# First slot of a hybrid decoder layer reordered, GpSimd given a share of its weight split, prefetch buffers re-laid

## The chip, the cores and the metric

The kernel runs on one core of a Trainium2 chip. The metric is device time in microseconds (us) from launch to end. The kernel before takes 1367.12 us, the median of 3 runs (1366.63 to 1367.73).

## What is computed

One decoder layer on 256 tokens of width 1024, in float32, then a mixture of experts (MoE) and a last RMSNorm. Cut to what matters here:

```
h = rmsnorm(x, norm_mix);  proj = h @ w_in                  # 1024 x 10256
y_ml = mLSTM(conv + silu of q,k; v; gates);  y_fx = forgetting attention
kv = rmsnorm(mem, norm_mem) @ w_mem_kv;      y_ca = attention of q into kv
x += (sum over b of sigmoid(gate_b) * (y_b @ w_branch[b])) @ w_out
t = rmsnorm(x, norm_moe);  top 4 of 32 experts by softmax router
for each expert:  u = t @ w1 + b1;  a = clamped SwiGLU(u);  out += weight * (a @ w2 + b2)
return rmsnorm(x, norm_final)
```

Each expert has 8 MB in `w_exp_in` and 4 MB in `w_exp_out`, 12 MB in all.

## The kernel before

Every engine has its own program, and semaphores join them. The work has two parts.

**Mixing.** The dense matmuls are 32 units of 512 weight columns (`UNITS`), each cut into 2 slots (`SLOTS`, 64 in all, numbered i). SyncE (SP) loads unit u into `ring[u % 3]`, 2 MB each. For accuracy each operand is split into a rounded part `hi` and a remainder `lo`, and three products are summed: hi·hi, hi·lo, lo·hi. For slot i ScalarE (ACT) writes `w_hi[i % 2]` (`round_weights`, L571), then VectorE (DVE) writes `w_lo[i % 2]` (`split_weights`, L870), then TensorE (PE) runs the slot (`project`: L1286 for slots of kind "T", L1297 for kind "N"). `round_weights(i)` waits until slot i-2 is done, because the two buffers alternate. Slot 0 goes down the list k = 0..7 with all three products of a k together. Beside the slots the dictionary `STAGES` hangs small pieces of work on slot numbers: `conv` and `conv_silu` on slots 0 to 7, `gate_weights` on slot 2, `gates` (PE, L1325) on slot 3, the attention heads later.

**The start.** SP loads x (2 transfers), small rows, unit 0 in two halves, three transfers of gate weights `wg`, three of biases, unit 1, `mem`, unit 2. ACT sums squares of x (`square_sums`, L545) and takes one Sqrt for both halves of tokens (L547). DVE takes reciprocals (L850), scales x into `xn` (`scale_rows`, L852) and copies `cols` (the norm weights, turned by PE at L1246). PE turns `xn` (`turn_rows`, L1233) into banks 4 to 7, ACT rounds them to `h_hi` (`round_turned`, L555), DVE forms `h_lo` (`split_turned`, L859). PE fills gaps with dummy matmuls (`keep_clock`, L1240). Right after slot 1's weights are rounded ACT sums the squares of `mem` (`square_sums(mems, ...)`), ahead of `round_weights(2)`. GpSimd (POOL) builds constants, at the end `pick` (a memset L489 and two `affine_select`, L493).

**MoE.** 10 buffers `place[0..9]` of 2 MB hold pieces of expert weights, 6 pieces to an expert: 4 of `w_exp_in` and 2 of `w_exp_out`, in turn. SP loads a piece (`load`, L390) once PE has used up the place (`place_used`). PE runs an expert at L1472/L1473 and adds results by L1557. The first 10 pieces are loaded ahead, during mixing. The places lie over the mixing buffers, so that each waits for the buffers under it to be dead: place 0 to 2 are the ring, place 3 is `fxkT` and `fxv`, and the layout order of `part(...)` decides the others.

Of the kernel before, what the change touches and what calls it, by code (L numbers as in the profile page):

```python
# [7 lines left out]
ALU = mybir.AluOpType  # L8
# [128 lines left out]
def build(nc, x, mem, norm_mix, w_in, b_ml_gates, conv_ml, ml_head_norm, b_fx_gate, norm_mem,  # L137
# [3 lines left out]
    with ctx:  # L141
# [117 lines left out]
        cF = part("cF", [12, S])  # L259
        big_f = part("big_f", [P, 2 * D])  # L260
        sig_o = big_f[:, :].rearrange("p (t d) -> p t d", t=TT)
        ycaT = big_f[:, :].rearrange("p (c s) -> p c s", c=KT)

        o_hi, o_lo = (part(f"o_{n}", [P, KT, S], F32R) for n in ("hi", "lo"))

        h_hi, h_lo = (part(f"h_{n}", [P, KT, S], F32R) for n in ("hi", "lo"))

        w_hi = [part(f"w_hi{n}", [P, KT, HW], F32R) for n in range(2)]
        w_lo = [part(f"w_lo{n}", [P, KT, HW], F32R) for n in range(2)]
        mixing.close()  # L270
# [103 lines left out]
        def _(sp):  # L374
# [5 lines left out]
            def load(e, j, b):  # L380
# [9 lines left out]
                sp.dma_start(place[b][:, :, :].rearrange("p k n -> p (k n)"), src).then_inc(place_in[b], 16)  # L390

            for u, (name, kind, j) in enumerate(UNITS):
                b = u % RING
                if u == 21:

                    sp.wait_ge(proj_done, FIRST["caq"] + 3)
                    load(0, RING, RING)
                if u == 25:

                    sp.wait_ge(proj_done, FIRST["caq"] + 11)  # L400
                    load(0, W1, W1)
# [63 lines left out]
        def _(pool):  # L465
# [65 lines left out]
        def _(act):  # L531
# [9 lines left out]
            def square_sums(src, n, loaded):  # L541

                for t in range(TT):
                    act.wait_ge(loaded[t], 16)
                    act.activation(square_dump[t], src[:, t, :], ACT.Square, accum_out=ss[:, t, 0:1]).then_inc(squares, 1)  # L545
                act.wait_ge(squares, 2 * n + 2)
                act.activation(std[:, :, 0:1], ss[:, :, 0:1], ACT.Sqrt, bias=eps[:, 0:1],  # L547
                               scale=1.0 / D).then_inc(std_ready, 1)

# [9 lines left out]
            def round_weights(i):  # L559
                if i >= len(SLOTS):  # L560
                    return
                u = UNIT_OF[i]
                if i == 0:
                    act.wait_ge(first_half_in, 16)
                else:
                    act.wait_ge(weights_in[u % RING], 16 * (u // RING + 1))
                if i >= 2:
# [271 lines left out]
        def _(dve):  # L839
# [8 lines left out]
            def scale_rows(src, dst, n):  # L848
                dve.wait_ge(std_ready, n + 1)
                step(dve.reciprocal(rstd[:, :, 0:1], std[:, :, 0:1]))  # L850
                for t in range(TT):
                    dve.tensor_scalar(dst[:, t, :], src[:, t, :], rstd[:, t, 0:1], None, ALU.mult).then_inc(scaled, 1)  # L852

# [11 lines left out]
            def split_weights(i):  # L865
                if i >= len(SLOTS):
                    return
                dve.wait_ge(weights_rounded, i + 1)
# [4 lines left out]
            scale_rows(xs, xn, 0)  # L873
# [188 lines left out]
            for i in range(len(SLOTS)):  # L1062
# [22 lines left out]
            dve.tensor_reduce(sq[:, :], ss[:, :, 0:2], AX.X, ALU.add).then_inc(sq_ready, 1)  # L1085
            dve.wait_ge(std_ready, 3)
            dve.reciprocal(rstd[:, :, 0:1], std[:, :, 0:1]).then_inc(rstd_ready, 1)
# [131 lines left out]
        def _(pe):  # L1219
# [7 lines left out]
            def turn_rows(src, user):  # L1227

                for q in range(4):
# [16 lines left out]
            pe.transpose(bank[7][:, 0:64], rows[:, :], ident[0:64, 0:64]).then_inc(filled[7], 1)  # L1246
            keep_clock(0, 8)
            pe.wait_ge(scaled, 2)
            turn_rows(lambda t, c: xn[:, t, P * c:P * (c + 1)], "x")
            keep_clock(0, 8)  # L1250
            def free_banks(i):
# [8 lines left out]
                else:  # L1260
                    pe.wait_ge(act_drained, act_drains(last))

            def project(i):
                name, kind, j, half = SLOTS[i]

                pe.wait_ge(weights_split, i + 1)
                free_banks(i)
                if j == 0 and half == 0:
# [324 lines left out]
```

## Time and profile before

| | |
|---|---|
| median of 3 runs | 1367.12 us |
| the profiled execution, its own time | 1366.06 us |
| its span, first to last instruction | 1364.3 us |
| PE busy | 1317.0 us, 97% of the span |
| DVE / ACT / POOL busy | 473.9 / 327.5 / 21.4 us |
| chain that ended last | PE 81%, DMA 13%, ACT 2%, DVE 1% |
| mean granted TensorE clock | 0.995 |
| traffic | 475.06 MB, mean 348 GB/s |

All times below are of that one execution, in us from the first instruction. A row of a timeline gives start, duration, engine, line and operation, count, and in brackets how long the engine had been idle and what released it. The mixing part runs to about 437, the experts from 448 to 1351.

### The profile page before, as it was taken

Reading aid. Unit: us, or ns where it says so; the run is one execution under the profiler, and the core shown is the slowest. Engines: PE = TensorE matmul, PEld = TensorE weight load, DVE = VectorE, ACT = ScalarE, POOL = GpSimd, SP = SyncE. Lnnn points to the kernel's source line nnn. Section 1 sums busy time; section 2 is a strip of 40 time slices with the busy share of each in tenths; the row PEclk is TensorE's granted clock in tenths of the full one; section 3 lists DMA queues with packets and bytes.
Section 4 is the critical chain, followed back from the end, with each engine's and each line's share of the span. In section 5 each row is a group of like instructions: output and inputs, shape, how many; then the busy total and the mean of one; then the engine's idle time right before and its main releaser. Section 6 shows DMA issues by size and latency. Waiting matters only on the chain.

```text
span 1364.3 us, 16054 instructions
## 1 busy us (share of the span) xinstructions
PE 1317.0 (97%) x6489; PEld 679.6 (50%) x6489; DVE 473.9 (35%) x802; ACT 327.5 (24%) x476; POOL 21.4 (2%) x39
## 2 busy tenths in 40 slices
PE   7999999999999999999999999999999999999995
PEld 7889997988888333333333333333333333333331
DVE  4754545444656322322223222322223222322223
ACT  5564545464444100110011000100011001110002
POOL 2000000000101000000000000000000000000000
PEclk9999999999999999999999999999999999999998
DMA  9354443545568999999999999999999999999993
GB/s 315 138 198 160 139 170 124 211 160 211 185 244 331 407 427 430 432 431 430 431 432 431 431 431 431 433 431 430 431 432 430 431 431 431 434 430 431 432 430 160
DMA packets 68233, 475.06 MB, mean 348 GB/s; under 512 B 8480, under 2 KB 10592, under 8 KB 43616
## 3 DMA queue, kind: packets, MB, share of 16 engines
q1 hardware_dynamic: 66048, 473.01, 83.7%
q10 hardware_dynamic: 2144, 1.47, 0.4%
q8 instruction: 29, 0.48, 0.1%
q14 instruction: 12, 0.10, 0.0%
HBM read 473.42 MB, written 1.05 MB: 348 GB/s over the span
## 4 chain that ended last, share of the span: by engine, by line
PE 81%; DMA 13%; ACT 2%; DVE 1%; SPq 1%; issue 1%; ACTq 0%; DVEq 0%
PE bank L1472 44%; PE bank L1297 17%; DMA place<-in_w_exp_in 12%; PE bank L1286 7%; PE bank L1557 4%; PE bank L1485 1%; ACT fxqT L808 1%; PE bank L1529 1%; PE bank L1501 1%; DMA fxv<-in_mem 1%; PE bank L1521 1%; PE bank L1473 1%; PE bank L1410 1%; PE bank L1429 1%; DVE w_lo L870 1%
## 5 line engine op out<-in xcount | busy, mean ns | idle before, releaser
L1472 PE MATMUL bank<-place,fxqT 128*64 128x512 f32 x1536 | 688.0, 597 | 22.1 <-ACT fxqT L808 15.6
L1473 PE MATMUL bank<-place,fxqT 128*64 128x512 f32 x1536 | 688.1, 597 | 0.0
L1472 PEld LDWEIGHTS bank<-place,fxqT 128*64 128x64 f32 x1536 | 199.2, 137 | 422.1 <-issue 389.6
L1148 DVE TENSOR_SCALAR big_a<-bank 128x512 f32<-128x512 f32 x32 | 22.1, 692 | 525.2 <-PE bank L1473 525.2
L870 DVE TENSOR_TENSOR w_lo<-ring,w_hi 128x2048 fp32r<-128x2048 f32 x64 | 146.7, 2291 | 153.5 <-ACT w_hi L571 153.3
L1473 PEld LDWEIGHTS bank<-place,fxqT 128*64 128x64 f32 x1536 | 199.2, 137 | 0.0
L571 ACT ACTIVATE w_hi<-ring 128x2048 fp32r<-128x2048 f32 x64 | 122.7, 1918 | 158.7 <-PE bank L1297 113.9
L805 ACT ACTIVATE big_a<-big_a 128x512 f32<-128x512 f32 x32 | 20.1, 630 | 435.3 <-DVE big_a L1148 435.3
L1176 DVE TENSOR_TENSOR xs<-bank,xs 128x512 f32<-128x512 f32 x132 | 81.9, 683 | 24.3 <-PE bank L1557 24.3
L1297 PE MATMUL bank<-w_hi,h_hi 128*128 128x512 f32 x224 | 88.3, 394 | 0.1
L1297 PE MATMUL bank<-w_hi,h_lo 128*128 128x512 f32 x224 | 87.3, 390 | 0.0
L1297 PE MATMUL bank<-w_lo,h_hi 128*128 128x512 f32 x224 | 87.2, 389 | 0.0
L815 ACT ACTIVATE p_a<-bank 128x512 f32<-128x512 f32 x32 | 19.1, 598 | 245.4 <-PE bank L1473 245.4
L1286 PE MATMUL bank<-h_hi,w_hi 128*128 128x256 f32 x256 | 74.2, 290 | 3.0 <-DVE w_lo L870 3.0
L1286 PE MATMUL bank<-h_hi,w_lo 128*128 128x256 f32 x256 | 73.1, 286 | 0.0
L1286 PE MATMUL bank<-h_lo,w_hi 128*128 128x256 f32 x256 | 73.1, 285 | 0.0
L1557 PE MATMUL bank<-p_a,fxqT 64*128 64x512 f32 x264 | 65.6, 615 | 0.8 <-ACT p_a L815 0.8
L1473 PE MATMUL bank<-big_c,sel 128*64 128x512 f32 x132 | 62.1, 592 | 0.0
L1472 PE MATMUL bank<-big_c,sel 128*64 128x512 f32 x132 | 62.1, 592 | 0.0
L1139 DVE TENSOR_TENSOR fxqT<-bank,g_rows 128x256 f32<-128x256 f32 x66 | 24.9, 419 | 95.0 <-PE bank L1485 95.0
L1286 PEld LDWEIGHTS bank<-h_hi,w_hi 128*128 128x128 f32 x256 | 49.8, 195 | 3.4 <-DVE w_lo L870 3.2
L1297 PE MATMUL bank<-w_hi,o_hi 128*128 128x512 f32 x128 | 51.0, 398 | 0.0
(269 smaller groups left out, 1272.6 us busy)
## 6 DMA issues: line engine op xcount, KB each, us to landing
place<-in_w_exp_in SPq DMA_DIRECT2D x128, 2048.0 KB, 28.2
place<-in_w_exp_out SPq DMA_DIRECT2D x64, 2048.0 KB, 28.5
ring<-in_w_in SPq DMA_DIRECT2D x19, 2048.0 KB, 7.6
ring<-in_w_branch SPq DMA_DIRECT2D x6, 2048.0 KB, 7.6
ring<-in_w_mem_kv SPq DMA_DIRECT2D x4, 2048.0 KB, 7.7
ring<-in_w_out SPq DMA_DIRECT2D x2, 2048.0 KB, 12.4
ring<-in_w_in SPq DMA_DIRECT2D x2, 1024.0 KB, 7.5
xs<-in_x SPq DMA_DIRECT2D x2, 512.0 KB, 4.3
```

Of the source, the lines that this page charges most:

```text
L571: act.activation(hi, whole, ACT.Copy).then_inc(weights_rounded, 1)
L805: act.activation(sig, gate, ACT.Sigmoid, scale=ALPHA).then_inc(sig_ready, 1)
L815: act.activation(yS, bank[5][:, :], ACT.Copy).then_inc(yS_ready, 1)
L870: dve.tensor_tensor(lo, whole, hi.bitcast(F32), ALU.subtract).then_inc(weights_split, 1)
L1139: dve.tensor_tensor(gotT[:, :, h, :], bank[3][:, :].rearrange("p (q h c) -> p q h c", q=4, h=2)[:, :, h, :], weights[:, :, h].unsqueeze(2) ...
L1148: dve.tensor_scalar(gate.rearrange("c (q p) -> c q p", q=4), bank[0][:, :].rearrange("c (p q) -> c q p", q=4), LIMIT, None, ALU.min).then_ ...
L1176: dve.tensor_tensor(dst, bank[b][:, :], dst, ALU.add).then_inc(put_added, 1)
L1286: ins = mm(bank[i % 4][:, S * c:S * (c + 1)], stationary, moving, start=(k == 0 and n == 0), stop=(k == KT - 1 and n == 2))
L1297: ins = mm(bank[2 * (UNIT_OF[i] % 2) + c][:, :], stationary, moving, start=(k == 0 and n == 0), stop=(k == KT - 1 and n == 2))
L1472: mm(o[0:CAP, :], lhsT, low, start=start, stop=stop)
L1473: return mm(o[CAP:P, :], lhsT, high, start=start, stop=stop)
L1557: mm(bank[b][:, :], selWT[half, t, :], yS[half, :], start=True, stop=True).then_inc(put_done, 1)
```

## The change

Seven edits:

1. On slot 0, DVE writes `w_hi` itself (`tensor_copy`), POOL writes the first half (k = 0..3) of `w_lo`, DVE the second half. ACT's first weight rounding is now that of slot 1. POOL's build of `pick` comes behind its new work.
2. `project_first`: PE runs slot 0 product by product: all hi·hi, then all with `h_lo`, then all with `w_lo`.
3. RMSNorm's Sqrt, reciprocal and scaling go by half of the tokens. `turn_x` turns the first half of the tokens for all 4 banks, then the second. Two runs of dummy matmuls go, one shrinks from 8 to 4.
4. `cols` is copied ahead of the scaling of x.
5. SP loads units 1 and 2 and `mem` ahead of `wg` and the biases.
6. The squares of `mem` (ACT) and its scaling (DVE) move to slot 3.
7. The mixing buffers are laid out anew: place 4 is now `big_b` and `big_f`, place 5 `o_hi`/`o_lo`, place 6 `h_hi`/`h_lo`, place 7 the weight buffers of even slots, place 8 those of odd slots, place 9 `big_e`, `pick` and the masks. The loads ahead follow: places 3, 9, 4, 2, 5, 0, 1, 7, 6, 8, where it was 3, 4, 5, 6, 2, 0, 1, 7, 8, 9.

The semaphores `weights_rounded` and `weights_split` no longer count slot 0, so the waits on them ask for one less.

DVE at the start, before (`w_lo0` is the buffer of slot 0, `w_lo1` that of slot 1; bank 7 holds the turned rows):

```order
L850 RECIPROCAL rstd<-std 128x2
L852 TENSOR_SCALAR big_a<-xs,rstd 128x1024 x2
L875 COPY cols<-bank7 128x64
L870 TENSOR_TENSOR w_lo0<-ring0,w_hi0 128x2048
L859 SCALAR_TENSOR_TENSOR h_lo<-bank4,cols,h_hi 128x256 x2
L859 SCALAR_TENSOR_TENSOR h_lo<-bank5,cols,h_hi 128x256 x2
L859 SCALAR_TENSOR_TENSOR h_lo<-bank6,cols,h_hi 128x256 x2
L859 SCALAR_TENSOR_TENSOR h_lo<-bank7,cols,h_hi 128x256 x2
L870 TENSOR_TENSOR w_lo1<-ring0,w_hi1 128x2048
```

and DVE at the start, of the change:

```order
L887 COPY cols<-bank7 128x64
L864 RECIPROCAL rstd<-std 128x1
L865 TENSOR_SCALAR big_a<-xs,rstd 128x1024
L864 RECIPROCAL rstd<-std 128x1
L865 TENSOR_SCALAR big_a<-xs,rstd 128x1024
L891 CAST w_hi0<-ring0 128x2048
L872 SCALAR_TENSOR_TENSOR h_lo<-bank4,cols,h_hi 128x256 x2
L872 SCALAR_TENSOR_TENSOR h_lo<-bank5,cols,h_hi 128x256 x2
L872 SCALAR_TENSOR_TENSOR h_lo<-bank6,cols,h_hi 128x256 x2
L872 SCALAR_TENSOR_TENSOR h_lo<-bank7,cols,h_hi 128x256 x2
L895 TENSOR_TENSOR w_lo0<-ring0,w_hi0 128x1024
L883 TENSOR_TENSOR w_lo1<-ring0,w_hi1 128x2048
```

The copy of `cols` moved up, the rounding of slot 0's weights came from ACT, and half of their remainder went behind `h_lo`.

SP's loads ahead of the experts, from the two loads of `w_out` (units 30 and 31) on, before:

```order
L415 DMA ring0<-in_w_out 128x8x512
L415 DMA ring1<-in_w_out 128x8x512
L390 DMA place6<-in_w_exp_in 128x4096
L390 DMA place2<-in_w_exp_in 128x4096
L390 DMA place0<-in_w_exp_in 128x4096
L390 DMA place1<-in_w_exp_in 128x4096
L390 DMA place7<-in_w_exp_in 128x4096
L390 DMA place8<-in_w_exp_in 128x4096
L390 DMA place9<-in_w_exp_in 128x4096
```

and there of the change:

```order
L422 DMA ring0<-in_w_out 128x8x512
L422 DMA ring1<-in_w_out 128x8x512
L391 DMA place2<-in_w_exp_in 128x4096
L391 DMA place5<-in_w_exp_out 128x4096
L391 DMA place0<-in_w_exp_in 128x4096
L391 DMA place1<-in_w_exp_in 128x4096
L391 DMA place7<-in_w_exp_in 128x4096
L391 DMA place6<-in_w_exp_in 128x4096
L391 DMA place8<-in_w_exp_in 128x4096
```

Seven pieces follow `w_out` in both; place 2 now goes first and no longer waits for slot 59, and place 7 waits for slot 62 where it waited for slot 63.

The diff, cut to its core:

```diff
+        big_f = part("big_f", [P, 2 * D])
 ...
+        o_hi, o_lo = (part(f"o_{n}", [P, KT, S], F32R) for n in ("hi", "lo"))
+        h_hi, h_lo = (part(f"h_{n}", [P, KT, S], F32R) for n in ("hi", "lo"))
+        w_parts = [[part(f"w_{n}{i}", [P, KT, HW], F32R) for n in ("hi", "lo")] for i in range(2)]
+        w_hi, w_lo = ([pair[n] for pair in w_parts] for n in range(2))
 ...
@@ SP @@
-                    load(0, RING, RING)
+                    load_ahead(3)
-                    load(0, W1, W1)
+                    load_ahead(9)
-                    load(0, W1 + 1, W1 + 1)
+                    load_ahead(4)
+                if u == RING:
+                    sp.wait_ge(first_low, 1)
                 if u >= RING:
-                    sp.wait_ge(weights_split, 2 * (u - RING) + 2)
+                    sp.wait_ge(weights_split, 2 * (u - RING) + 1)
 ...
-                if u == 0:
+                if u == 2:
                     wv = w_in[0].rearrange("(k p) n -> p k n", p=P)
                     sp.dma_start(wg[:, :, 0:4], wv[:, :, C_F:C_F + 4]).then_inc(gatew_in, 16)
 ...
+            last = len(UNITS) - 1
+            sp.wait_ge(weights_split, SLOT_OF[last - 2, 1])
+            load_ahead((last - 2) % RING)
             sp.wait_ge(proj_done, FIRST["b2"] + 4)
-            load(1, 0, PIECES)
-            for u in range(len(UNITS) - RING, len(UNITS)):
-                sp.wait_ge(weights_split, SLOT_OF[u, 1] + 1)
-                load(0, u % RING, u % RING)
+            load_ahead(5)
+            for u in (last - 1, last):
+                sp.wait_ge(weights_split, SLOT_OF[u, 1])
+                load_ahead(u % RING)
+            sp.wait_ge(proj_done, len(SLOTS) - 1)
+            load_ahead(7)
             sp.wait_ge(proj_done, len(SLOTS))
-            for j in range(1, W1):
-                load(1, j, PIECES + j)
+            load_ahead(6)
+            load_ahead(8)
@@ POOL @@
+            pool.wait_ge(rows_zero, 4)
+            pool.wait_ge(first_rounded, 1)
+            whole, hi, lo = slot_weights(0)
+            pool.tensor_tensor(lo[:, 0:KT // 2, :], whole[:, 0:KT // 2, :], hi[:, 0:KT // 2, :].bitcast(F32),
+                               ALU.subtract).then_inc(first_low, 1)
+            pool.wait_ge(first_low, 1)
             pool.memset(pick[:, :, :].bitcast(F32), 0.0).then_inc(pick_built, 1)
@@ ACT @@
-                act.wait_ge(squares, 2 * n + 2)
-                act.activation(std[:, :, 0:1], ss[:, :, 0:1], ACT.Sqrt, bias=eps[:, 0:1],
+                    act.wait_ge(squares, 2 * n + t + 1)
+                    act.activation(std[:, t, 0:1], ss[:, t, 0:1], ACT.Sqrt, bias=eps[:, 0:1],
 ...
-            round_weights(0)
 ...
-            act.wait_ge(scaled, 2)
-            square_sums(mems, 1, [mem_in, mem_in])
 ...
+                if i == 3:
+                    square_sums(mems, 1, [mem_in, mem_in])
@@ DVE @@
+            scale_rows(xs, xn, 0)
+            dve.wait_ge(first_half_in, 16)
+            whole, hi, lo = slot_weights(0)
+            dve.tensor_copy(hi, whole).then_inc(first_rounded, 1)
 ...
+            dve.tensor_tensor(lo[:, KT // 2:KT, :], whole[:, KT // 2:KT, :], hi[:, KT // 2:KT, :].bitcast(F32),
+                              ALU.subtract).then_inc(first_high, 1)
 ...
-                if i == 1:
+                if i == 3:
                     scale_rows(mems, mems, 1)
@@ PE @@
-            keep_clock(0, 8)
-            pe.wait_ge(scaled, 2)
-            turn_rows(lambda t, c: xn[:, t, P * c:P * (c + 1)], "x")
-            keep_clock(0, 8)
+            keep_clock(0, 4)
+            turn_x()
 ...
+            def project_first():
+                whole, wh, wl = slot_weights(0)
+                pe.wait_ge(first_rounded, 1)
+                for n, (stationary, moving) in enumerate(((wh, h_hi), (wh, h_lo), (wl, h_hi))):
+                    for k in range(KT):
+                        q, user = k // 2, ("x", k // 2)
+                        if n == 0 and k % 2 == 0:
+                            pe.wait_ge(turned_rounded, q + 1)
+                        if n == 1 and k % 2 == 0:
+                            pe.wait_ge(drained[4 + q], turn(4 + q, user))
+                        if n == 2 and k in (0, KT // 2):
+                            pe.wait_ge(first_high if k else first_low, 1)
```

## Rows read from the trace of the kernel before

**Rows 1.** Windows: us, busy PE, PEld, DVE, ACT, POOL, clock, DMA share, GB/s.

```profile
31.20:446.88 415.68, 412.31 (x2308) 356.76 (x2308) 230.37 (x295) 210.66 (x277) 11.89 (x17) 1.00 0.53 192
```

**Rows 2.** Waits of PE, up to 446 and from 1106: total, times, longest.

```profile
PE bank L1286 <- DVE w_lo L870: 3.0, 1, 3.0
PE bank L1325 <- DVE o_lo L939: 2.3, 1, 2.3
...
PE bank L1472 <- DMA place<-in_w_exp_in: 6.5, 6, 1.1
```

**Rows 3.** The chain of waits, the experts: start, duration, what.

```profile
464.99 1.92 PE bank L1557 x8
...
1106.36 1.92 PE bank L1557 x8
...
1337.45 1.92 PE bank L1557 x8
```

**Rows 4.** Windows around the first expert.

```profile
452.00:454.00 2.00, 2.00 (x12) 0.63 (x10) 0.00 (x0) 0.00 (x0) 0.00 (x0) 1.00 0.75 188
454.00:456.00 2.00, 2.00 (x11) 0.56 (x7) 0.00 (x0) 0.00 (x0) 0.00 (x0) 1.00 0.64 229
456.00:466.00 10.00, 10.00 (x47) 3.40 (x48) 2.77 (x4) 1.23 (x2) 0.00 (x0) 1.00 1.01 433
```

**Rows 5.** SP's queue: two issues of its timeline, and its waits.

```profile
436.27 1.28 SPq L390 DMA_DIRECT2D place<-in_w_exp_in  x3
452.62 0.35 SPq L390 DMA_DIRECT2D place<-in_w_exp_out  x1
...
SPq L390 <- PE bank L1473: 764.2, 182, 14.7
```

**Rows 6.** Timeline of all engines, the start.

```profile
6.88 0.25 PE L1246 MATMUL bank<-ident,rows 64*128 64x64 f32 x1 [1.14 <-DMA rows<-in_conv_ml]
7.19 3.49 POOL L493 TENSOR_SCALAR_AFFINE_SELECT pick<-pick 64x1536 fp32r<-64x1536 f32 x2
7.32 0.30 ACT L547 ACTIVATE std<-ss,eps 128x2 f32<-128x2 f32 x1
7.85 3.38 DVE L852 TENSOR_SCALAR big_a<-xs,rstd 128x1024 f32<-128x1024 f32 x2
9.24 1.91 ACT L571 ACTIVATE w_hi<-ring 128x2048 fp32r<-128x2048 f32 x1 [1.62 <-DMA ring<-in_w_in]
11.29 3.50 PE L1233 MATMUL bank<-ident,big_a 128*128 128x128 f32 x16 [2.19 <-DVE big_a L852]
12.33 3.33 ACT L555 ACTIVATE h_hi<-bank,cols 128x256 fp32r<-128x256 f32 x8 [1.18 <-PE bank L1233]
13.61 3.22 DVE L859 SCALAR_TENSOR_TENSOR h_lo<-bank,cols,h_hi 128x256 fp32r<-128x256 f32 x8
```

**Rows 7.** ACT's timeline, then the chain of waits.

```profile
24.51 1.06 ACT L545 ACTIVATE fxkT<-fxv 128x1024 f32<-128x1024 f32 x1 [7.04 <-DMA fxv<-in_mem]
...
31.21 7.52 PE bank L1286 x48
...
101.01 5.75 PE bank L1286 x48
```

**Rows 8.** DVE's and POOL's prices: timelines, and a group of DVE's lines.

```profile
37.48 1.42 DVE L852 TENSOR_SCALAR fxv<-fxv,rstd 128x1024 f32<-128x1024 f32 x2
...
428.78 2.40 POOL L519 TENSOR_TENSOR b1split<-b1raw,b1split 32x1024 fp32r<-32x1024 f32 x1 [59.53 <-ACT b1split L782]
...
L870 DVE TENSOR_TENSOR w_lo<-ring,w_hi 128x2048 fp32r<-128x2048 f32 x64 | 146.7, 2291 | 153.5 <-ACT w_hi L571 153.3
```

**Rows 9.** Windows of 2 us in which the granted clock matters.

```profile
12.00:14.00 2.00, 2.00 (x12) 2.00 (x11) 2.00 (x2) 1.66 (x5) 0.00 (x0) 0.50 0.32 10
...
32.00:34.00 2.00, 2.00 (x12) 2.00 (x11) 1.93 (x6) 0.90 (x1) 0.00 (x0) 0.50 0.96 261
...
46.00:48.00 2.00, 1.22 (x10) 1.22 (x11) 1.97 (x4) 1.49 (x3) 0.00 (x0) 1.00 0.00 0
```

More of the change, by code:

```diff
@@ L245, in build @@
         big_b = part("big_b", [P, 2 * D])
+        big_f = part("big_f", [P, 2 * D])
+        sig_o = big_f[:, :].rearrange("p (t d) -> p t d", t=TT)
+        ycaT = big_f[:, :].rearrange("p (c s) -> p c s", c=KT)
+        o_hi, o_lo = (part(f"o_{n}", [P, KT, S], F32R) for n in ("hi", "lo"))
+        h_hi, h_lo = (part(f"h_{n}", [P, KT, S], F32R) for n in ("hi", "lo"))
+        w_parts = [[part(f"w_{n}{i}", [P, KT, HW], F32R) for n in ("hi", "lo")] for i in range(2)]
+        w_hi, w_lo = ([pair[n] for pair in w_parts] for n in range(2))
         caqT = big_b[:, :].rearrange("p (c s) -> p c s", c=KT)
@@ L259, in build @@
         cF = part("cF", [12, S])
[L260 to L269, printed above, removed]
         mixing.close()
@@ L278, in build @@
         first_half_in = sem("first_half_in")
+        first_rounded, first_low, first_high = sem("first_rounded"), sem("first_low"), sem("first_high")
         weights_rounded, weights_split = sem("weights_rounded"), sem("weights_split")
@@ L390, in load, with load_ahead @@
                 sp.dma_start(place[b][:, :, :].rearrange("p k n -> p (k n)"), src).then_inc(place_in[b], 16)
+            def load_ahead(b):
+                load(b // PIECES, b % PIECES, b)
             for u, (name, kind, j) in enumerate(UNITS):
@@ L545, in square_sums @@
                     act.activation(square_dump[t], src[:, t, :], ACT.Square, accum_out=ss[:, t, 0:1]).then_inc(squares, 1)
-                act.wait_ge(squares, 2 * n + 2)
-                act.activation(std[:, :, 0:1], ss[:, :, 0:1], ACT.Sqrt, bias=eps[:, 0:1],
-                               scale=1.0 / D).then_inc(std_ready, 1)
+                    act.wait_ge(squares, 2 * n + t + 1)
+                    act.activation(std[:, t, 0:1], ss[:, t, 0:1], ACT.Sqrt, bias=eps[:, 0:1],
+                                   scale=1.0 / D).then_inc(std_ready, 1)
             def round_turned(hi, user, g):
@@ L562, in round_weights @@
                 u = UNIT_OF[i]
[L563 to L566, printed above, removed]
+                act.wait_ge(weights_in[u % RING], 16 * (u // RING + 1))
                 if i >= 2:
@@ L848, in scale_rows @@
             def scale_rows(src, dst, n):
-                dve.wait_ge(std_ready, n + 1)
-                step(dve.reciprocal(rstd[:, :, 0:1], std[:, :, 0:1]))
                 for t in range(TT):
+                    dve.wait_ge(std_ready, 2 * n + t + 1)
+                    step(dve.reciprocal(rstd[:, t, 0:1], std[:, t, 0:1]))
                     dve.tensor_scalar(dst[:, t, :], src[:, t, :], rstd[:, t, 0:1], None, ALU.mult).then_inc(scaled, 1)
@@ L867, in split_weights @@
                     return
-                dve.wait_ge(weights_rounded, i + 1)
+                dve.wait_ge(weights_rounded, i)
                 whole, hi, lo = slot_weights(i)
@@ L1085, in _ @@
             dve.tensor_reduce(sq[:, :], ss[:, :, 0:2], AX.X, ALU.add).then_inc(sq_ready, 1)
-            dve.wait_ge(std_ready, 3)
+            dve.wait_ge(std_ready, 5)
             dve.reciprocal(rstd[:, :, 0:1], std[:, :, 0:1]).then_inc(rstd_ready, 1)
@@ L1235, in turn_rows, with turn_x @@
                     ins.then_inc(filled[4 + q], 1)
+            def turn_x():
+                for t in range(TT):
+                    pe.wait_ge(scaled, t + 1)
+                    for q in range(4):
+                        if t == 0:
+                            claim(4 + q, ("x", q))
+                        for c in range(2):
+                            ins = pe.transpose(bank[4 + q][:, S * c + P * t:S * c + P * (t + 1)],
+                                               xn[:, t, P * (2 * q + c):P * (2 * q + c + 1)], ident[:, :])
+                        if t == TT - 1:
+                            ins.then_inc(filled[4 + q], 1)
             def keep_clock(b, times):
@@ L1261, in free_banks @@
                     pe.wait_ge(act_drained, act_drains(last))
+            def project_first():
[10 more added lines that the diff above has]
+                            pe.wait_ge(first_high if k else first_low, 1)
+                        for c in range(2):
+                            ins = mm(bank[0][:, S * c:S * (c + 1)], stationary[:, k, P * c:P * (c + 1)], moving[:, k, :],
+                                     start=(n == 0 and k == 0 and c == 0),
+                                     stop=(n == 2 and k == KT - 1 and c == 1))
+                ins.then_inc(proj_done, 1)
             def project(i):
                 name, kind, j, half = SLOTS[i]
-                pe.wait_ge(weights_split, i + 1)
+                if i:
+                    pe.wait_ge(weights_split, i)
                 free_banks(i)
@@ L1273, in project @@
                         pe.wait_ge(o_split, {"b1": 1, "b2": 2}[name])
+                if i == 0:
+                    return project_first()
                 hi, lo = (o_hi, o_lo) if name in ("mk", "mv", "b0", "b1", "b2") else (h_hi, h_lo)
@@ L1279, in project @@
                         for k in range(KT):
-                            if i == 0 and c == 0 and k % 2 == 0:
-                                pe.wait_ge(drained[4 + k // 2], turn(4 + k // 2, ("x", k // 2)))
                             passes = [(wh[:, k, tile], hi[:, k, :]), (wh[:, k, tile], lo[:, k, :]),
```

3 lines of the change are left out of this document (1 added, 2 removed).

## The prediction

> **What bounds the kernel now.** I read the windows by stage first, then PE's waits, then the chain of waits, then the queue of transfers. From 31 to 447 PE is busy 412.3 of 415.7 us [rows 1]: mixing is bound by PE, and before 446 PE waits inside it only twice, 3.0 us for a `w_lo` and 2.3 us for `gates` [rows 2]. Nothing that the change does to loads in mixing can be felt there, for PE never waits for a ring load.
>
> The experts have two limits. From 464.99 to 1106.36 lie 23 experts at 27.89 us: PE's pace. From there to 1337.45 are 8 at 28.89 us [rows 3]: 8.0 us more than PE needs, and in that stretch PE waits for places [rows 2]. A piece is 2.097 MB and the transfers run at 433 GB/s [rows 4], so 4.84 us a piece and 29.1 us an expert. The transfers are slower than PE all along, and PE lives on its 10 places until they are used up. So the end hangs on a line of transfers. Where does it start? SP waited 182 times for a place to be used up [rows 5], 192 pieces less the 10 loaded ahead. The first of the 182 is issued at 452.62, when PE has used the first piece of expert 0, and data flow again only about 2.3 us later: the windows from 452 to 456 carry 188 and 229 GB/s in place of 433 [rows 4]. 182 pieces at 4.84 from 454.9 end at 1336, at a rate 0.6% lower at 1341: the last expert. The end is thus the first release of a place plus a constant, and the release follows PE. What PE gains in mixing is handed on whole, in both limits.
>
> **The fill order (edit 7): 0 us.** Ten pieces are loaded ahead in both versions. One of them (place 2) goes earlier by the wait for slot 59, one is left to SP's last wait less: after slot 63 come 2 pieces in place of 3 [rows 5]. The fill is over one piece, 4.8 us, earlier, at 448 instead of 453. But the 11th piece has no place until 452.62, and PE waits for none of the ten: the only waits for a place are those from 1106 on [rows 2]. So the queue idles 4.8 us more before the release, and nothing moves. Bounds: 0 and -4.8 us. I take 0.
>
> **The start, step by step.** Before, slot 2 begins at 31.21 after a wait of 3.0 [rows 2, 7], so slot 1 ended at 28.2 and began, at 5.75 us a slot [rows 7], at 22.4. What will that be now?
>
> *Scaling of x.* The two scalings took 3.38 us, and those of `mem`, the same shape, 1.42 [rows 6, 8]. In between lies POOL: its two selects for `pick` ran from 7.19 to 10.68 [rows 6]. They now come behind POOL's share of the weights, so I take 0.71 each. The rows land by 6.88 and the PE turn of them takes 0.25 [rows 6]; `cols` is copied by 7.4; two reciprocals with their waits (0.2 each) and two scalings end at 9.3. The second half's root is there at 7.62 [rows 6], in time. Before: 11.23.
>
> *Turning and `h_hi`.* The second half's transposes start at 9.3, the first bank is full at about 9.6. ACT's 8 roundings take 3.33 [rows 6]: `h_hi` is whole at 12.95, the four quarters coming from 10.5 on. Before: 15.66.
>
> *DVE.* The first half of unit 0 is there at 9.24 [rows 6]. The rounding on DVE, 2048 wide, is in no row: at the pace of the scaling (0.71 for 1024) 1.3 us, at that of the subtraction 2.29 [rows 8]. It is a one-source operation like the scaling, so 1.3: 9.3 to 10.6. Then `h_lo`, 8 at 0.40 = 3.22 [rows 6], the last quarter bound to `h_hi`: done at 13.75. Half a subtraction, 1.2: 14.95. ACT rounds slot 1's weights from 12.95 to 14.86. DVE's whole subtraction for slot 1, 2.29 [rows 8]: 17.25.
>
> *POOL.* Its half of `w_lo`: the row with 1024 elements a partition took 2.40 [rows 8]; even twice that, from 10.6, ends by 15.4, when PE asks. Hidden.
>
> *PE.* hi·hi follows the quarters and ends at 13.5; 16 products are a third of 5.75, 1.92: with `h_lo` to 15.4, with `w_lo` to 17.3. So PE and DVE are ready for slot 1 together at 17.3, if DVE meets nobody.
>
> *Where it meets somebody.* POOL ends its subtraction at 13.0, clears `pick` until 14.4 and then has its two selects, 3.49 us [rows 6], just when DVE subtracts. The row of the scaling shows what a meeting costs: 3.38 less 1.42 is 1.96 for two selects met, 0.98 each; a whole select is 1.75. DVE is within its half subtraction when the select asks, so the select comes next and DVE's whole subtraction waits for it. The Trainium skill (SBUF — State Buffer, Who interferes with whom) has this as a rule: the pair of ports that DVE and GpSimd share is held for a whole instruction, and a DVE operation with two SBUF inputs contends with a GpSimd one that reads SBUF. The trace agrees for the scaling: 1.69 where 0.71 was due. It speaks against this change, which puts the selects beside the subtractions; without it the sum would be 1.4 larger in gain. I take 1.4 for one select met (between 0.98 and 1.75), bounds 0 and 3.5: slot 1 begins at 18.7. Gain: 22.4 - 18.7 = 3.7 us.
>
> *Slot 2.* It waited because ACT, ahead of `round_weights(2)`, sat until 24.5 for `mem` [rows 7]. That is moved to slot 3. Now ACT rounds when slot 0 is done: 17.3 + 1.9 + 2.3 = 21.5, slot 1 ends at 24.45. Unit 1 must have landed by 20.2; its 2.1 MB stand behind 1.05 MB at 9.24, at 433 GB/s 16.5. Gain 3.0 us. After that wait the granted clock fell to 0.50 [rows 9], and slot 2 took 7.52 in place of 5.75 [rows 7]: gain 1.8.
>
> *Slots 3 to 7.* `gates` keeps its 2.3: it follows the end of slot 2 by ACT's rounding, DVE's subtraction, a `conv` and `gate_weights`, none changed. The squares of `mem` with two table loads, some 6 us of ACT, and the scaling, 1.8 of DVE, lie in slot 3 and `gates`, where ACT next has a rounding due only after slot 4, some 11 us on. Free; with that cover gone up to 2. `wg` now lands behind unit 2, some 25 to 28, and is asked for at 31. Free.
>
> **Sum.** 3.7 + 3.0 + 1.8 = 8.5 us. Against the profiled execution's own 1366.06 (span 1364.3) that is 1357.6; the median of the runs shown is 1.06 above it, so 1358.6.
>
> **Rivals.**
>
> *A, the fill counts after all.* Then the tail also gives 4.8: 1353.8. For it: transfers do bound the end. Against it: SP's 182 waits are all for PE [rows 5]. Chance 0.06.
>
> *B, the dense order keeps the engines apart worse than I think*, or the rounding takes 2.29 and both selects are met, or the clock falls once more. The clock fell for some 3.4 us after PE idled 2.2 before 11.29 [rows 6, 9] and 3.0 before slot 2, but not after the 2.3 before `gates` [rows 2, 9]; a fall costs 1.8. Together 1 + 2.1 + 1.8 less gain: 3.6, so 1363.5. Chance 0.12 for 1361 or more, still faster.
>
> *C, slower: the queue serves its transfers side by side.* Units 1 and 2 and `mem` now stand behind unit 0 from 4 us on. If they share, 1.05 + 1.05 + 2.1 + 1.05 + 2.1 MB run together, and the first half lands not at 9.24 but at about 19. DVE's chain from there (1.3, 3.2, 1.2, 2.3) puts slot 1 at 27.3, 4.9 later than before; less the 4.8 of slot 2, plus 1.4 for the select: 1368.6. It decides from a landing after 17.9, where the gain is gone. Against it: before, the second half of unit 0 already stood behind the first, and the first was there at 9.24. The Trainium skill (DMA: Bandwidth & Descriptors, Queues, rings and completion order) says that each engine takes a ring's descriptors in order; by that C is excluded, and no row here shows so deep a queue at the start. Chance 0.03.
>
> *D, nothing gained:* a wait in slots 3 to 7 that takes it back. Chance 0.02 within 0.2%, which is about 2.7 us and what a measurement of this kernel can tell from no change.
>
> **How the numbers follow.** The forecast, gain 7 to 10, has 0.77: its own range is 1356.5 to 1360.5. With the bounds of the select (0 and 3.5), of the rounding and of the clock the range is 1355.8 to 1362. Faster 0.95, same 0.02, slower 0.03.
>
> **What would show it.** In the profile after: x scaled by 9.3 with two scalings of 0.7; slot 1 at 17.3 to 19.5, and a select of POOL between DVE's two subtractions; no wait of PE and no clock of 0.50 before slot 2; `gates` still waiting 2.3; the queue idle longer before the first release, which comes some 8.5 earlier; experts at 27.9 and then 28.9 to 29.1 as before. It is wrong if the tail is shorter by more than the start is (A), or if slot 0's weights land after 12.

## The result, and the profile after

The changed kernel takes 1357.04 us (median of 4 runs, 1356.08 to 1358.92) beside 1367.42 of before in the same runs: ratio 0.9926, interval 0.9912 to 0.994. Forecast was 1358.6, a gain of 8.5 us; the medians differ by 10.4 (the interval is 8.2 to 12.0), the two profiled spans by 9.4 (1364.3 and 1354.9). Run again, beside other kernels, it took 1358.21 where before took 1367.08: 8.9 us (ratio 0.993, 0.9914 to 0.9947).

The windows of mixing and the waits of PE (TensorE) up to 446, after, against [rows 1, 2]:

```profile
31.20:437.34 406.14, 402.73 (x2244) 347.26 (x2243) 224.60 (x286) 211.57 (x282) 12.98 (x17) 1.00 0.55 201
```

```profile
PE bank L1373 <- DVE o_lo L957: 2.3, 1, 2.3
PE bank L1271 <- POOL eps L479: 1.1, 1, 1.1
PE bank L1306 <- DVE w_hi L891: 0.9, 1, 0.9
...
PE bank L1334 <- DVE w_lo L883: 0.3, 1, 0.3
```

The 3.0 us before slot 2 are gone, the 2.3 before `gates` stand. The start, where the change is: timeline of all engines, after, against [rows 6].

```profile
6.67 0.25 PE L1277 MATMUL bank<-ident,rows 64*128 64x64 f32 x1 [0.85 <-DMA rows<-in_conv_ml]
7.29 0.76 DVE L865 TENSOR_SCALAR big_a<-xs,rstd 128x1024 f32<-128x1024 f32 x1
8.10 1.97 PE L1263 MATMUL bank<-ident,big_a 128*128 128x128 f32 x16
8.15 0.75 DVE L865 TENSOR_SCALAR big_a<-xs,rstd 128x1024 f32<-128x1024 f32 x1
9.51 3.03 ACT L573 ACTIVATE h_hi<-bank,cols 128x256 fp32r<-128x256 f32 x8 [2.06 <-PE bank L1263]
9.73 1.23 DVE L891 CAST w_hi<-ring 128x2048 fp32r<-128x2048 f32 x1 [0.82 <-DMA ring<-in_w_in]
10.87 3.22 DVE L872 SCALAR_TENSOR_TENSOR h_lo<-bank,cols,h_hi 128x256 fp32r<-128x256 f32 x8
11.11 2.42 POOL L504 TENSOR_TENSOR w_lo<-ring,w_hi 128x1024 fp32r<-128x1024 f32 x1 [5.39 <-DVE w_hi L891]
14.01 1.22 DVE L895 TENSOR_TENSOR w_lo<-ring,w_hi 128x1024 fp32r<-128x1024 f32 x1
15.12 5.41 POOL L511 TENSOR_SCALAR_AFFINE_SELECT pick<-pick 64x1536 fp32r<-64x1536 f32 x2
15.14 2.28 DVE L883 TENSOR_TENSOR w_lo<-ring,w_hi 128x2048 fp32r<-128x2048 f32 x1
17.62 1.92 ACT L586 ACTIVATE w_hi<-ring 128x2048 fp32r<-128x2048 f32 x1 [3.23 <-DMA ring<-in_w_in]
19.57 3.10 DVE L883 TENSOR_TENSOR w_lo<-ring,w_hi 128x2048 fp32r<-128x2048 f32 x1 [2.15 <-ACT w_hi L586]
```

Each scaling of x takes 0.75 us where two took 3.38. POOL's two selects take 5.41 where they took 3.49: now it is POOL that stands back. The chain of waits goes on, after, against [rows 7]:

```profile
17.48 11.79 PE bank L1334 x96
...
37.32 3.14 PE bank L1373 x24
```

Slots 1 to 3 run without a gap and at full clock. `gates` starts at 37.32; before it was 46.78, so 9.5 us are won by there. By the first matmul of each slot, 4.8 of them are won before slot 1 (22.29 and now 17.48), 3.1 between slots 1 and 2 (31.21 and 23.33), and 1.6 within slot 2 (slot 3 at 38.55 and 29.09). Last, SP's queue, the windows round the first release and the experts in the chain of waits, after, against [rows 3 to 5]:

```profile
443.12 3.73 SPq L391 DMA_DIRECT2D place<-in_w_exp_out  x2
...
SPq L391 <- PE bank L1521: 764.7, 182, 15.3
```

```profile
440.00:442.00 2.00, 2.00 (x12) 0.71 (x10) 0.00 (x0) 0.00 (x0) 0.00 (x0) 1.00 0.15 57
442.00:444.00 2.00, 2.00 (x12) 0.58 (x10) 0.00 (x0) 0.00 (x0) 0.00 (x0) 1.00 0.00 0
444.00:446.00 2.00, 2.00 (x12) 0.58 (x8) 0.00 (x0) 0.00 (x0) 0.00 (x0) 1.00 1.04 270
```

```profile
455.50 1.92 PE bank L1605 x8
...
1096.86 1.92 PE bank L1605 x8
...
1328.31 1.92 PE bank L1605 x8
```

The first release of a place comes at 443.12, 9.50 us earlier. The bulk of the fill is over by about 440.3 (an estimate: the 57 GB/s of 440 to 442 are 0.3 us at the full rate), nothing moves from 442 to 444, and so the queue idles ahead of the release: the time won by the new fill order lies there, unused. 23 experts go at 27.89 us, the last 8 at 28.93, where before they took 27.89 and 28.89.

### The profile page after: what moved, and what is told of

It is laid out like the page before. It is cut to its first block, busy times and chain, and to the rows that moved or that the text cites. A ratio compares the mean times of both kernels' runs of the same rounds, so it can differ in the third digit from the quotient of the medians.

```text
span 1354.9 us, 16014 instructions
## 1 busy us (share of the span) xinstructions
PE 1311.5 (97%) x6465; PEld 673.9 (50%) x6465; DVE 473.3 (35%) x805; ACT 328.4 (24%) x479; POOL 26.9 (2%) x40
## 4 chain that ended last, share of the span: by engine, by line
PE 85%; DMA 10%; ACT 2%; DVE 2%; issue 1%; SPq 0%; DVEq 0%; ACTq 0%
PE bank L1520 46%; PE bank L1345 17%; DMA place<-in_w_exp_in 9%; PE bank L1334 7%; PE bank L1605 4%; PE bank L1533 1%; ACT fxqT L821 1%; PE bank L1577 1%; PE bank L1549 1%; PE bank L1569 1%; PE bank L1521 1%; PE bank L1458 1%; PE bank L1477 1%; DMA ring<-in_w_in 1%; DVE w_lo L883 0%
## 5 line engine op out<-in xcount | busy, mean ns | idle before, releaser
L818 ACT ACTIVATE big_a<-big_a 128x512 f32<-128x512 f32 x32 | 20.2, 631 | 435.7 <-DVE big_a L1166 435.7
L1334 PE MATMUL bank<-h_hi,w_hi 128*128 128x256 f32 x240 | 68.8, 287 | 0.3 <-DVE w_lo L883 0.3
L1334 PE MATMUL bank<-h_lo,w_hi 128*128 128x256 f32 x240 | 67.9, 283 | 0.0
L1334 PE MATMUL bank<-h_hi,w_lo 128*128 128x256 f32 x240 | 67.9, 283 | 0.0
L1345 PE MATMUL bank<-w_hi,o_lo 128*128 128x512 f32 x128 | 49.9, 390 | 0.0
```

The costliest lines, as they stand in the source:

```text
L818: act.activation(sig, gate, ACT.Sigmoid, scale=ALPHA).then_inc(sig_ready, 1)
L1334: ins = mm(bank[i % 4][:, S * c:S * (c + 1)], stationary, moving, start=(k == 0 and n == 0), stop=(k == KT - 1 and n == 2))
L1345: ins = mm(bank[2 * (UNIT_OF[i] % 2) + c][:, :], stationary, moving, start=(k == 0 and n == 0), stop=(k == KT - 1 and n == 2))
```

## The experiments

The theory: mixing is bound by PE and its start by DVE's chain; what is won up to the first release of a place is handed on whole, since the time from there to the end is a constant. The rivals: the fill order counts (A), collisions and a slow clock eat the gain (B), deep queues delay the start (C). Each experiment is one kernel; "before" and "changed" in its edit say what it starts from.

Read the first release and the span side by side, from SP's timeline and the head of each profile. A slot and `gates` start with their first matmul, which overlaps the last one ahead of it by some 0.17 us where PE does not wait:

| kernel | slot 1 starts | `gates` starts, lasts | first release | span | difference |
|---|---|---|---|---|---|
| before | 22.29 | 46.78, 3.14 | 452.62 | 1364.3 | 911.7 |
| changed | 17.48 | 37.32, 3.14 | 443.12 | 1354.9 | 911.8 |
| e1 | | 48.07, 3.13 | 453.71 | 1365.3 | 911.6 |
| e2 | | 40.79, 4.63 | 448.09 | 1359.8 | 911.7 |
| e3 | 18.77 | 38.62, 4.49 | 445.74 | 1357.2 | 911.5 |
| e4 | | 42.40, 4.44 | 449.70 | 1361.8 | 912.1 |
| e5 | 20.21 | 40.05, 4.64 | 447.29 | 1359.0 | 911.7 |
| e6 | 17.29 | 34.66, 3.04 | 441.49 | 1353.1 | 911.6 |
| e7 | 17.89 | 37.73, 3.14 | 443.53 | 1346.9 | 903.4 |
| e8 | 19.28 | 39.02, 4.35 | 446.34 | 1358.3 | 912.0 |
| e9 | 17.42 | 34.79, 3.04 | 441.09 | 1353.0 | 911.9 |
| e10 | 17.55 | 37.39, 3.12 | 443.16 | 1354.9 | 911.7 |
| changed again | 17.01 | 36.85, 4.41 | 444.15 | 1356.5 | 912.4 |

With the same transfers (all but e7), twelve spans are the first release plus 911.5 to 912.4 us, over releases that lie 12.6 us apart.

### e1: the fill order alone

```diff
 # before, with edit 7: the parts laid out as in the change, and
-load(1, 0, PIECES) ... load(0, u % RING, u % RING) ... load(1, j, PIECES + j)
+load_ahead: places 3, 9, 4, 2, 5, 0, 1, 7, 6, 8
```

> The kernel before with edit 7 alone (layout of the mixing buffers and order of the loads ahead). Theory: the tail hangs on the first release of a place, so 0 us: first release at 452.6 as before, span 1364.3 within 1 us, while the fill ends some 4.8 us earlier and the queue idles that much longer. Rival A (the fill counts): the release stays and the tail shortens by 4.8 us, span 1359.5.

Measured: 1367.15 us (10 runs) beside 1367.33, ratio 0.9996, interval 0.9986 to 1.0006. Rival A's 4.8 us would be 0.9965 and lies outside. The windows of e1 round its first release at 453.71:

```profile
450.00:452.00 2.00, 2.00 (x10) 0.61 (x10) 0.00 (x0) 0.00 (x0) 0.00 (x0) 1.00 0.56 229
452.00:454.00 2.00, 2.00 (x12) 0.72 (x10) 0.00 (x0) 0.00 (x0) 0.00 (x0) 1.00 0.00 0
454.00:456.00 2.00, 2.00 (x12) 0.68 (x10) 0.00 (x0) 0.00 (x0) 0.00 (x0) 1.00 0.75 156
```

By the same estimate the bulk of the fill ends at about 451.1, 2.6 us ahead of the release, where before it ended 0.3 behind it [rows 4]. So against the release it is 2.9 us earlier, not 4.8 as I had said. Nothing comes of it: A falls. The release of this execution is 1.1 later than before because slot 2 began 0.4 later and took 8.45 us in place of 7.52, more of it at half clock.

### e2: the squares of mem alone

```diff
 # before
-            act.wait_ge(scaled, 2)
-            square_sums(mems, 1, [mem_in, mem_in])
 ...
+                if i == 3:
+                    square_sums(mems, 1, [mem_in, mem_in])
-                if i == 1:
+                if i == 3:
                     scale_rows(mems, mems, 1)
```

> The kernel before with edit 6 alone (squares and scaling of mem moved to slot 3). Theory: the 3.0 us wait before slot 2 goes, the clock of 0.50 in it too (1.8 us): slot 2 starts at 28.2 and lasts 5.75, gates 4.8 us earlier (42.0), span 1359.5. Rival: the moved work is not covered in slot 3 and takes back up to 2 us, as a new wait of PE before slots 5 to 7: span 1361.5.

Measured: 1362.48 (6 runs) beside 1367.33, ratio 0.9969, interval 0.9957 to 0.9982: 4.8 us. Chain of waits of e2:

```profile
15.02 17.71 PE bank L1287 x144
...
40.79 4.63 PE bank L1326 x24
```

Three slots in one piece, no wait and no slow clock in slot 2. `gates` starts 6.0 earlier, not 4.8, because the transposes here met no slow clock (1.96 in place of 3.50), and then lasts 1.5 longer at half clock. The release comes 4.5 earlier. The size is right in this profile partly by luck: two effects of the clock, which I had not foreseen, cancel.

### e3: pick built first

```diff
 # changed, POOL
+            (memset and two selects of pick)
             pool.wait_ge(rows_zero, 4)
             pool.wait_ge(first_rounded, 1)
             pool.tensor_tensor(lo[:, 0:KT // 2, :], ...)
-            (memset and two selects of pick)
```

> The changed kernel with POOL's build of pick back ahead of its share of slot 0's weights. Theory (exclusive use of a port by POOL's selects and DVE's scaling): the two scalings of x meet the two selects and end near 11.0 in place of 8.8; DVE rounds slot 0's weights from 11.0 in place of 9.7, everything behind it 1.3 us later, slot 1 at 18.8, span 1356.2. Rival (no meeting, the scaling was slow before for another reason, as its two halves under one root): scalings 0.75 each, slot 1 at 17.5, span 1354.9.

Measured: 1359.13 (3 runs), slot 1 at 18.77 where 18.8 was expected. DVE and POOL in e3:

```profile
7.06 0.75 DVE L865 TENSOR_SCALAR big_a<-xs,rstd 128x1024 f32<-128x1024 f32 x1
7.92 1.84 DVE L865 TENSOR_SCALAR big_a<-xs,rstd 128x1024 f32<-128x1024 f32 x1
9.87 2.38 DVE L891 CAST w_hi<-ring 128x2048 fp32r<-128x2048 f32 x1
```

```profile
7.18 3.99 POOL L505 TENSOR_SCALAR_AFFINE_SELECT pick<-pick 64x1536 fp32r<-64x1536 f32 x2
```

The first scaling, begun 0.1 us ahead of the select, takes 0.75. The second (1.84) and the rounding (2.38 in place of 1.23) each wait for a select. I had expected both scalings to be met and to end near 11.0; they end at 9.77, and the rounding is met in their place, so that 18.8 came out right by another way. Moving `pick` is worth 1.3 us. The release is 2.6 us later than in the changed kernel; the rest of that is `gates` at half clock, 4.49 in place of 3.14.

### e4: gate loads first

```diff
 # changed, SP
-                if u == 2:
+                if u == 0:
                     wv = w_in[0].rearrange("(k p) n -> p k n", p=P)
```

> The changed kernel with SP's wg and bias loads back ahead of unit 1. Theory: unit 1 is issued at 13.1 and lands near 20.5; ACT rounds 20.5 to 22.4, DVE is done at 24.7 or 25, slot 1 ends at 23.3: PE waits 1.5 us before slot 2, span 1356.4. The first half of unit 0 lands at 9.24 again and not at 9.71, which takes up to 0.5 off slot 1. Rival (the order of the loads is free): span 1354.9 or 0.5 less.

Measured: 1361.47 (7 runs), span 1361.8. ACT's timeline of e4:

```profile
22.66 1.91 ACT L586 ACTIVATE w_hi<-ring 128x2048 fp32r<-128x2048 f32 x1 [7.94 <-DMA ring<-in_w_in]
```

Unit 1 lands at 22.6, 2 us later than I had worked out. It was issued at 13.90, 0.8 later than I took; and `mem` and unit 2 stand right behind it, of which some 0.6 MB is through before it is whole (2.7 MB in all moved on the queue between its issue and its landing). Slot 2 starts 3.6 us later than in the changed kernel, after two waits of 3.6 us for DVE in all, and has half clock for most of its length, which costs 1.5 (slot 3 starts 5.1 later); `gates` falls too, 4.44 in place of 3.14. 3.6 + 1.5 + 1.3 = 6.4, and the release is 6.58 later. So SP's order is worth 3.6 us to the new start, and in this profile a slow clock of 1.5 came with it. The first half of unit 0 did not land sooner (10.04), against my expectation: over the profiles it lands anywhere from 8.6 to 10.1, in either order.

### e5: DVE splits slot 0 alone

```diff
 # changed
-            pool.tensor_tensor(lo[:, 0:KT // 2, :], ...).then_inc(first_low, 1)
-            dve.tensor_tensor(lo[:, KT // 2:KT, :], ...).then_inc(first_high, 1)
+            dve.tensor_tensor(lo, whole, hi.bitcast(F32), ALU.subtract).then_inc(first_high, 1)
```

> The changed kernel with DVE doing the whole w_lo of slot 0 (POOL's subtraction left out, its other work where it was). Theory: DVE's chain is what slot 1 waits for, and grows by half a subtraction, 1.15 us: slot 1 at 18.6, span 1356.0. Rival (PE's own work sets slot 1, POOL's share is not on the path): slot 1 at 17.5, span 1354.9.

Measured: 1360.9 (4 runs), slot 1 at 20.21 where 18.6 was expected. DVE and POOL in e5:

```profile
14.32 2.29 DVE L891 TENSOR_TENSOR w_lo<-ring,w_hi 128x2048 fp32r<-128x2048 f32 x1
16.53 3.63 DVE L879 TENSOR_TENSOR w_lo<-ring,w_hi 128x2048 fp32r<-128x2048 f32 x1
```

```profile
12.92 5.10 POOL L507 TENSOR_SCALAR_AFFINE_SELECT pick<-pick 64x1536 fp32r<-64x1536 f32 x2
```

This is the meeting that the prediction priced at 1.4. The first select took 1.54 and ended at 14.46. The second began at 14.61, within DVE's first subtraction, waited for it some 1.9 us and went next, and the second subtraction took 3.63 in place of 2.29, 1.34 more. With half a subtraction (1.07) and a landing 0.31 later that is 2.72 of the 2.73 us of slot 1. DVE's chain is the path, and POOL's share of it is worth its 1.1 us.

### e8: slot 0 by k

```diff
 # changed, project_first
-                for n, (stationary, moving) in enumerate(((wh, h_hi), (wh, h_lo), (wl, h_hi))):
-                    for k in range(KT):
+                for k in range(KT):
+                    for n, (stationary, moving) in enumerate(passes):
```

> The changed kernel with slot 0 in the order of before, all three products of a k together. Theory: the first k needs h_lo (11.7) and POOL's half of w_lo (13.5), so PE does the first half of slot 0 from 13.5 and the second from DVE's half at 15.1: slot 0 ends at about 19.3 in place of 17.2, slot 1 right behind it at 19.3, 1.8 us later, span 1356.7. Rival (the order by product is worth nothing, DVE's chain bounds slot 1 at 17.4 anyway): span 1354.9.

Measured: 1359.75 (3 runs), slot 1 at 19.28, as the theory said, but not for its reason alone. PE's timeline of e8:

```profile
12.42 0.50 PE L1307 MATMUL bank<-h_hi,w_lo 128*128 128x256 f32 x2 [0.72 <-POOL w_lo L504]
...
14.55 0.63 PE L1307 MATMUL bank<-h_hi,w_lo 128*128 128x256 f32 x2
...
17.60 0.40 PE L1307 MATMUL bank<-h_hi,w_lo 128*128 128x256 f32 x2
```

The third product waits for POOL as expected, but from 13.2 to 16.6 the clock is at half (a pair 0.63 us in place of 0.40), which costs 1.7. Without it slot 1 would have begun near 17.6, 0.6 later than in the changed kernel run again. Whether the short waits of this order bring the fall about, or chance did, stays open; so does the worth of the order by product, between 0.6 and 2.3 us.

### e7: fewer bytes

```diff
 # changed, SP's load(): inside the loop, w_exp_out by half
+                if j >= W1 and not isinstance(e, int):
+                    sp.dma_start(place[b][:, 0:KT // 4, :]..., src[:, 0:KT // 4 * 2 * UW])
```

> The changed kernel, but each piece of w_exp_out that is loaded inside SP's loop is transferred by half (the other half of the place keeps older values, so part of the expert sum is computed from other weights). Theory: transfers bound the last 8 experts; with 5 pieces' bytes for an expert (24.2 us) they bound nowhere, all 32 experts go at PE's 27.9 us, and the end comes 8 us earlier: span 1347, no wait of PE for a place. Rival: the last experts are slow for a reason in PE's own work: span 1355, the same 28.9 us.

This kernel leaves half of each such piece untransferred. Measured: 1348.68 (2 runs), span 1346.9, release plus 903.4. Chain of waits of e7, two experts at the end of the run:

```profile
1292.42 1.92 PE bank L1609 x8
1320.28 1.92 PE bank L1609 x8
```

These two are the last expert but one and the last: 27.86 us, and PE waits for no place from 1100 on. The 8.4 us by which the tail is shorter are what transfers cost the last 8 experts.

### e6 and e9: two versions that beat both

```diff
 # e6: changed, gate_weights ahead of conv on slot 2
+_stage(2, "gate_weights")
 for _i in range(4):
     _stage((0, 2, 4, 6)[_i], "conv", _i)
     _stage((1, 3, 5, 7)[_i], "conv_silu", _i)
-_stage(2, "gate_weights")
```

> The changed kernel with DVE's gate_weights ahead of conv(1) in slot 2. Theory: PE's wait of 2.3 us before gates is the time of conv(1) in front of the remainder of wg; it goes, gates start when slot 3 ends (35.0 in place of 37.3), and the 2.3 us are handed on whole to the first release and to the end: span 1352.6 against 1354.9, faster than both kernels. Rival: the tail of transfers does not follow the release, and the experts' gain is lost there: span 1354.9. Second rival: conv(1) later makes split 5 or the gates work late, gain under 1.5.

Measured: 1354.99 (4 runs), ratio 0.9911 (0.9894 to 0.9927), span 1353.1. The wait before `gates` is gone, the release 1.63 earlier, the end 1.8. The ratios of e6 and of the changed kernel overlap in their intervals; what tells them apart is the profile, and e9 below, which ran beside the changed kernel. Of the 2.3 us 0.7 are back as a new wait, before slot 6; chain of waits of e6:

```profile
41.35 1.28 ACT L627
...
43.31 0.04 DVE merged L951
...
46.97 2.30 DVE w_lo L883
...
49.31 11.35 PE bank L1345 x48
```

The squares of `mem` and their table loads hold ACT, then DVE's `conv_silu`, its gate work, the scaling of `mem` and the subtraction for slot 6. The prediction called edit 6 free and named 2 us for a lost cover; here the cover has shrunk by 2.3 us and the lack of it costs 0.7.

```diff
 # e9: e6, with mem at slot 8 for ACT and DVE
-                if i == 3:
+                if i == 8:
```

> The version of e6 (gate_weights ahead of conv(1)) with the squares and the scaling of mem moved on from slot 3 to slot 8. Theory: e6 kept 0.7 us of its 2.3 us in a new wait before slot 6, since the squares of mem with their two table loads stand ahead of conv_silu(1) on ACT and so ahead of DVE's gates work, scaling and split 6. With that work at slot 8, where DVE idles some 3 us a slot, the wait goes: span 1352.4 against 1353.1, median near 1354.2. Rival (the wait is due to conv(1) and gates alone): 0.7 us wait stays, span 1353.1.

Measured: 1354.75 (4 runs, 1354.41 to 1355.09; the changed kernel beside it 1356.89 to 1358.54), ratio 0.9907 (0.9891 to 0.9924), span 1353.0. The wait before slot 6 is gone: PE runs slots 4 to 7 in one piece from 37.67 on. So its cause was the squares of `mem`, as I had said. A wait of 0.28 us stands elsewhere, before slot 11 at 76.84: there the subtraction comes right behind the scaling of `mem` (two of 0.75 us, up to 74.6), which now lies in its way. The release came 0.4 earlier, and e9 can't be told from e6 by time.

### e10 and the changed kernel again: the clock before gates

```diff
 # e10: changed, PE in gates()
-                pe.wait_ge(wg_split, 2)
                 claim(4, ("gates", 0))
+                keep_clock(4, 9)
+                pe.wait_ge(wg_split, 2)
```

> The changed kernel with 9 dummy matmuls of 128 columns in PE's wait before gates (2.3 us). Theory: the idle of PE there makes the granted clock fall to 0.50 in some executions and not in others (it fell in five profiles, gates then took 4.4 to 4.6 us in place of 3.14); with PE busy it never falls: gates 3.14, span 1354.9, and the runs lie close together, as those of e6 (within 0.5 us), near 1356.6, where those of the changed kernel spread over 2.8 us. Rival: the fall comes from something else: gates at 4.5 again in the profile or the same spread.

> The changed kernel once more, beside the two others on one chip. Theory: release at 443 to 445, span minus release 911.7 as in all kernels so far; if the clock falls before gates the span is 1356.3, if not 1354.9. DVE's split of slot 1 may meet POOL's select (slot 1 at 18.8) or not (17.5): they asked for the port within 0.1 us of one another.

Measured: e10 1356.26 (1355.18 to 1356.95), the changed kernel beside it 1358.21 (1356.89 to 1358.54). A window of the changed kernel run again, then one of e10:

```profile
38.00:40.00 2.00, 2.00 (x13) 2.00 (x12) 1.00 (x1) 1.97 (x4) 0.00 (x0) 0.56 0.37 144
```

```profile
38.00:40.00 2.00, 2.00 (x20) 2.00 (x19) 1.54 (x1) 1.97 (x4) 0.00 (x0) 1.00 0.97 378
```

The same program had clock 1.00 there in its first profile and 0.56 in its second, `gates` 3.14 and 4.41. With PE kept busy it is 1.00 and 3.12. Of ten profiles with the wait of 2.3 us the clock fell to 0.50 in or behind it in six (e2, e3, e4, e5, e8, the changed kernel again); of three in which PE idles there 0.3 us or not at all (e6, e9, e10) in none. The runs of e10 spread by 1.8 us, not by 0.5 as I expected, and its median is 2.0 below that of the changed kernel, more than the 1.2 to 1.5 that a fall costs: the fall explains the profiles, not the whole spread. In the changed kernel run again slot 1 started at 17.01, and POOL's first select began 0.28 us ahead of DVE's whole subtraction. DVE and POOL there:

```profile
13.54 1.21 DVE L895 TENSOR_TENSOR w_lo<-ring,w_hi 128x1024 fp32r<-128x1024 f32 x1
14.67 2.28 DVE L883 TENSOR_TENSOR w_lo<-ring,w_hi 128x2048 fp32r<-128x2048 f32 x1
```

```profile
14.39 5.66 POOL L511 TENSOR_SCALAR_AFFINE_SELECT pick<-pick 64x1536 fp32r<-64x1536 f32 x2
```

The subtraction runs at its full pace all the same.

## Why the prediction was right

**What bounds the kernel: right.** "The end is the first release of a place plus a constant" holds over twelve profiles to 0.9 us, through gains and losses, and e7 shows that transfers make the tail.

**The fill order, 0: right.** The profiles of the changed kernel and of e1 show the queue idle ahead of the release, and e1 shows no gain. The 0 was read from SP's 182 waits, all for PE [rows 5], and not from the share of DMA in the chain. That the fill would end 4.8 us earlier was wrong, it is some 3; nothing hung on it.

**The start.** Rounding 1.3 (1.23), POOL's half 2.40 (2.42), half a subtraction 1.2 (1.22): these durations came out of rows of before to 0.1 us, the one that no row showed too. The two ends, scaling by 9.3 (8.9) and `h_hi` by 12.95 (12.5), were each 0.4 late. One small term was missing: DVE idled 0.82 us for the first half of unit 0, which landed at 9.7, not at 9.24.

**The meeting with a select, 1.4: the step that failed.** It measured 0. The premise held: POOL's first select began within DVE's half subtraction (15.12, in 14.01 to 15.23). The step from there, "so the select comes next and DVE's whole subtraction waits for it", did not: the whole subtraction, begun at 15.14, ran first at its full 2.28, and the first select took 3.72 us in place of 1.54. A later subtraction met the second select and took 3.10, under cover. In all eight profiles with this work of POOL (the changed kernel twice, e4, e6 to e10) the first select begins 0.02 to 0.59 us ahead of the whole subtraction, and in all eight the subtraction goes first. It is thus no matter of a tenth in my sum: in e8 the select began at 13.95, 0.59 ahead of it, and waited for both subtractions. In e5 alone, after a wait of some 1.9 us, the select went between two of them; the price there, 1.34, was right. The Trainium skill (SBUF — State Buffer, Who interferes with whom) says that the holder keeps the shared ports for a whole instruction, and that issue order decides who blocks. e3 and e5 agree with the first (a scaling of 1.84, a subtraction of 3.63). The second does not account for e8 and the changed kernel run again, if a select asks when its record begins, and no run shows when it asks. Which of two waiting instructions is served next stays open, so such a term should have stood as 0 or 1.4, not as 1.4. With it gone (-1.4), the rounding of slot 0 at 9.73 in place of 9.3 (+0.4) and the chain behind it 0.2 shorter, slot 1 starts 1.2 us earlier than forecast (17.48, not 18.7).

**Slot 2, 3.0 + 1.8: right**, with 3.1 + 1.6 measured, and e2 gives 4.8 between the medians by itself. Unit 1 landed at 17.6, 1.1 later than worked out, within the cover to 20.2. e4 shows that this cover was thin: without edit 5 it is the next wait.

**`gates` keeps its 2.3: right.** That the clock may fall there was in rival B, at 1.8; it costs 1.2 to 1.5 and comes in six of the ten profiles, so it was not a mishap but a term with its own chance. The profile of the changed kernel had no fall there and gives a gain of 9.4 against 1364.3; its second one had one, and gives 7.8. That 8.5 lies between the two is luck: the missing 1.4 of the select and such a fall are about as large and go against each other.

**C: excluded here.** The first half of unit 0 landed at 9.7 with three transfers behind it. They do share a little (e4), some 0.6 MB, not half. The durations given for C add up to 27.0, not 27.3; nothing hangs on it.

## What to carry to other kernels

When the tail is bound by a line of transfers, find the event that starts the line and put every gain and loss against it: earlier loads that end before that event are worth nothing, and time won ahead of it is worth all of itself. Price collisions of DVE and GpSimd for a port from a row where they met, and where no row shows which of two waiting instructions goes first, keep both outcomes. Once the first slots run without a gap, the next wait of PE (here 2.3 us behind a `conv` that could stand after it) is the cheapest gain left.

## What had not been expected of the hardware

SP takes longer to issue a transfer when much stands in its queue. Timeline of SP, after:

```profile
4.19 2.69 SPq L422 DMA_DIRECT2D ring<-in_w_in  x1
6.92 2.73 SPq L432 DMA_DIRECT2D fxv<-in_mem  x1
...
10.92 6.01 SPq L425 DMA_DIRECT2D wg<-in_w_in  x1
16.96 6.49 SPq L426 DMA_DIRECT2D wg<-in_w_in  x1
```

In e4 the 2 MB load of unit 1, issued at 13.90 when the queue was all but empty, took 0.39 us to issue, and the three `wg` transfers 2.6 to 3.2 each behind unit 0. Behind units 0 to 2 and `mem`, 7.3 MB in all, the same three took 6.01, 6.49 and 3.45 and held SP until 27, and unit 3 was issued at 28.25 where its place was free at 17.4. PE had cover for it. What holds SP is not shown; the two orders of the same transfers are all that the runs compare.
